# Two transformer blocks on one core: feed-forward stages in two phases, two matmuls per weight tile, later ada sums

## The reference

```python
def rmsnorm(x, g):
    y = xf * lax.rsqrt(jnp.mean(xf * xf, axis=-1, keepdims=True) + EPS)
def swiglu(h, w_in, w_out):                  # w_in 1024 x 5632, w_out 2816 x 1024
    a, b = jnp.split(h @ w_in, 2, axis=-1)
    return (jax.nn.silu(a) * b) @ w_out
...
x = x + 0.5 * swiglu(rmsnorm(x, g[0]), ffn_w_in[layer, 0], ffn_w_out[layer, 0])
```

```python
ada = c_act @ w_ada[l] + b_ada[l]            # 1024 x 6144 weights for one row
sh1, sc1, gt1, sh2, sc2, gt2 = [t[:, None, :] for t in jnp.split(ada, 6, axis=-1)]
...
u = x * (1.0 + sc2) + sh2
h = jnp.square(jax.nn.relu(u @ w_up[l])) @ w_down[l]
x = layer_norm(DN_ALPHA * x + (1.0 + gt2) * h, ln_ffn_g[l], ln_ffn_b[l])
```

## Time and profile before

| | us |
|---|---|
| median of 3 runs (lowest, highest) | 2049.49 (2048.72, 2058.34) |
| the profiled execution, its own time | 2051.69 |
| its span | 2050.0 |
| TensorE busy, weight loads busy | 1924.4, 1826.6 |
| VectorE, ScalarE, GpSimd busy | 1331.9, 919.0, 772.9 |
| mean granted clock of TensorE | 0.937 |

### The profile page before, as it was taken

How to read it: one execution, slowest core, us unless ns; L and a number is a source line. 1 busy time by engine, 2 the same in 40 slices (tenths; PEclk the granted TensorE clock), 3 DMA queues, 4 the chain that set the end, 5 groups by cost and what they waited for, 6 DMA issues and landing times.

```text
span 2050.0 us, 34772 instructions
## 1 busy us (share of the span) xinstructions
PE 1924.4 (94%) x14460; PEld 1826.6 (89%) x14460; DVE 1331.9 (65%) x1393; ACT 919.0 (45%) x1168; POOL 772.9 (38%) x392
## 2 busy tenths in 40 slices
PE   7999999889989999989799989998999899989998
PEld 7999896789989999875699988888999898889997
DVE  6876544567677767465677757966655579666554
ACT  5433454344334433444344334674544456645443
POOL 3967200136666657012346683950000039400000
PEclk9999896789999999895899999999999999999999
DMA  7878351356875777430367754434455444345551
GB/s 234 266 228 268 100 165 62 103 171 225 266 251 165 246 247 245 144 103 1 103 206 248 243 189 144 133 115 144 144 184 184 144 145 145 104 144 166 184 183 42
DMA packets 288106, 347.61 MB, mean 170 GB/s; under 512 B 15060, under 2 KB 263688, under 8 KB 288008
## 3 DMA queue, kind: packets, MB, share of 16 engines
q1 hardware_dynamic: 287976, 346.18, 52.2%
q10 hardware_dynamic: 32, 0.02, 0.0%
HBM read 345.11 MB, written 1.07 MB: 169 GB/s over the span
## 4 chain that ended last, share of the span: by engine, by line
PE 84%; DVE 9%; ACT 3%; issue 2%; SPq 1%; DMA 1%; DVEq 0%; ACTq 0%
PE bank L765 24%; PE bank L766 24%; PE bank L767 24%; DVE wl L1597 2%; PE bank L940 2%; ACT wh L1244 2%; PE bank L963 2%; PE bank L951 1%; PE bank L802 1%; PE bank L1140 1%; PE bank L1201 1%; DVE xl L1608 1%; DVE xn L1628 1%; DVE hl L1658 1%; DMA raw<-in_ffn_w_in 1%
## 5 line engine op out<-in xcount | busy, mean ns | idle before, releaser
L1597 DVE TENSOR_TENSOR wl<-raw,wh 128x2048 fp32r<-128x2048 f32 x275 | 729.1, 2656 | 390.3 <-ACT wh L1244 390.0
L765 PE MATMUL bank<-xh,wh 128*128 128x256 f32 x3056 | 886.2, 290 | 67.3 <-DVE xl L1608 34.6
L766 PE MATMUL bank<-xl,wh 128*128 128x256 f32 x3056 | 877.9, 287 | 0.0
L767 PE MATMUL bank<-xh,wl 128*128 128x256 f32 x3056 | 877.3, 287 | 0.0
L1244 ACT ACTIVATE wh<-raw 128x2048 fp32r<-128x2048 f32 x275 | 524.9, 1909 | 400.8 <-PE bank L767 381.3
L765 PEld LDWEIGHTS bank<-xh,wh 128*128 128x128 f32 x3056 | 599.8, 196 | 83.5 <-issue 51.2
L766 PEld LDWEIGHTS bank<-xl,wh 128*128 128x128 f32 x3056 | 600.4, 196 | 0.4 <-issue 0.2
L767 PEld LDWEIGHTS bank<-xh,wl 128*128 128x128 f32 x3056 | 599.8, 196 | 0.0
L707 POOL TENSOR_TENSOR arena<-arena,csil 128x2048 f32<-128x2048 f32 x48 | 190.8, 3975 | 507.3 <-DMA arena<-in_w_ada 488.0
L765 PE MATMUL bank<-hh,wh 128*128 128x256 f32 x1216 | 347.4, 286 | 17.0 <-DVE hl L1658 17.0
L767 PE MATMUL bank<-hh,wl 128*128 128x256 f32 x1216 | 347.1, 285 | 0.0
(11 more groups left out here) (254 smaller groups left out, 1659.7 us busy)
## 6 DMA issues: line engine op xcount, KB each, us to landing
raw<-in_ffn_w_in SPq DMA_DIRECT2D x88, 1024.0 KB, 5.8
arena<-in_w_ada SPq DMA_DIRECT2D x48, 1024.0 KB, 7.5
raw<-in_ffn_w_out SPq DMA_DIRECT2D x44, 1024.0 KB, 5.1
raw<-in_w_in SPq DMA_DIRECT2D x36, 1024.0 KB, 5.0
raw<-in_w_up SPq DMA_DIRECT2D x32, 1024.0 KB, 5.7
raw<-in_w_down SPq DMA_DIRECT2D x32, 1024.0 KB, 4.9
raw<-in_even_w_in SPq DMA_DIRECT2D x12, 1024.0 KB, 5.3
raw<-in_w_out SPq DMA_DIRECT2D x8, 1024.0 KB, 5.3
```

The lines of the kernel that those rows point to most:

```text
L765: pe.matmul(o, wa, ma, start=start, stop=False, **kw)
L766: pe.matmul(o, wa, mb, start=False, stop=False, **kw)
L767: return pe.matmul(o, wb, ma, start=False, stop=stop, **kw)
L1597: dve.tensor_tensor(wl[:, c % RING, :], raw[:, c % RING, :], wh[:, c % RING, :].bitcast(F32), ALU.subtract).then_inc(lo_made.sem, 1)
```

## The change

It rewrites the feed-forward stages and what touches them.

1. xh and xl become the halves of one tensor xx (k, half, token), and the split hidden values go to a tensor hx (22 or 32 tiles, two halves) which lies where the arena begins. A weight tile takes two matmuls (`pair`): the low weights times the high half (256 columns), and the high weights times both halves at once (512 columns). Results fill the left and the right half of a bank.
2. The right halves must be added: ScalarE copies them out (L1339, L1344), VectorE adds the left halves from PSUM (L1700, L1703), then product, and split into hx.
3. All up chunks of a stage come first, then the down chunks in four groups of 256 output columns (8 + 8 + 6 tiles of k in ffn, 8 + 8 + 8 + 8 in sq). After a group VectorE adds the left and then the right halves to x; ScalarE squares these two tiles of x, and TensorE adds them to the norm's sums after the second chunk of the next group (`pe_stats`), so that 2 of 8 remain for the end.
4. `pool_ada` starts when the last xl of the norm is made. The ada chunks are loaded in steps 1 to 6, 8 and 10 and one with each down group, so the last later than before. The rope inputs are loaded after all hl and ada sums of ffn3.
5. `fetch` runs a small activation so that the table for Sqrt or Silu is there before its use.
6. In the odd stage chunk 0, small and chunk 1 come before the transposes of wuk, and wuk is loaded there. The constants of the even stage move out of the arena. The clearing of hpad moves from the rope stage into the mix stage. PE waits in ffn2 for ada_made before its second chunk.

The other stages keep `three`.

```diff
@@ pe_ffn
+            def pair(o, k, hi_w, lo_w, halves, start, stop):
+                pe.matmul(o[:, 0:T], lo_w, halves[:, 0, :], start=start, stop=False, skip_group_check=True)
+                return pe.matmul(o.rearrange("p (h t) -> p h t", h=2), hi_w, halves, start=False, stop=stop, skip_group_check=True)
...
                 if st > 0:
-                    pe.wait_ge(h_made.sem, shifted(h_made.at(s, 2 * st), turn, 2 * body))
+                    pe.wait_ge(a_made.sem, shifted(a_made.at(s, st), turn, STEP_BODY))
+                up(c, st, turn, 4)
+                if st > 0:
+                    pe.wait_ge(b_made.sem, shifted(b_made.at(s, st), turn, STEP_BODY))
+                elif s == "ffn2":
+                    pe.wait_ge(ada_made.sem, ada_made.at("ffn1"))
+                up(c + 1, st, turn, 6)
...
+            for g, j, c, k0, n in down_chunks(s):
+                pe.wait_ge(lo_made.sem, c + 1)
+                if g == 0:
+                    pe.wait_ge(hl_made.sem, hl_made.at(s, min(4 * (j + 1), steps)))
+                if g >= 2 and j == 0:
+                    pe.wait_ge(x_ready.sem, x_ready.at(s, 2 * (g - 1)))
+                for m in range(2):
+                    for k in range(n):
+                        last = pair(bank[2 * (g % 2) + m], k0 + k, *tile_of(c, k, m, T), hx[:, k0 + k, :, :],
+                                    start=(k0 + k == 0), stop=(j == len(DOWN[KIND[s]]) - 1 and k == n - 1))
+                last.then_inc(chunk_used.sem, 1)
+                if g >= 1 and j == 1:
+                    pe_stats(NEXT[s], range(2 * g - 2, 2 * g))
@@ pool_ada
+            moving = {"ffn0": "rms0", "ffn1": "rms2", "ffn2": "rms3", "ffn3": "rms5"}[s]
+            pool.wait_ge(xl_made.sem, xl_made.at(moving))
@@ act_rms
+        def fetch(func):
+            act.activation(early[:, :], epsc[:, 0:1], func)
...
+            if s != "rms0":
+                fetch(ACT.Sqrt)
...
+            if KIND[NEXT[s]] == "ffn":
+                fetch(ACT.Silu)
@@ act_ffn
+                act.wait_ge(chunk_used.sem, shifted(c + 1, turn, per))
+                act.activation(ra, psum[:, 4:6, T:2 * T], ACT.Copy).then_inc(right_out.sem, 1)
                 hi(c + RING, turn, per)
+                act.wait_ge(a_made.sem, shifted(a_made.at(s, st + 1), turn, STEP_BODY))
+                act.activation(fs, ra, ACT.Silu).then_inc(act_made.sem, 1)
+                act.wait_ge(chunk_used.sem, shifted(c + 2, turn, per))
+                act.activation(rb, psum[:, 6:8, T:2 * T], ACT.Copy).then_inc(right_out.sem, 1)
+                hi(c + 1 + RING, turn, per)
+                act.wait_ge(h_made.sem, shifted(h_made.at(s, st + 1), turn, STEP_BODY))
+                act.activation(hx[:, mine, 0, :], fh, ACT.Copy).then_inc(hh_made.sem, 1)
@@ odd stage
-    ODD = ["wuk", 0, "small", 1, "index", 2, "csq", "top", 3, "cnorm", "top", 4, "top", "K", 5, "top", "V", "mask", 6]
+    ODD = [0, "small", 1, "wuk", "index", 2, "csq", "top", 3, "cnorm", "top", 4, "top", "K", 5, "top", "V", "mask", 6]
@@ rope stage, vector
-                dve.wait_ge(rope_made.sem, 4)
-                dve.memset(hpad[:, :, 0:CONV_K - 1], 0.0)
```

More of the change, by code:

```diff
@@ L445, in att_of, with steps_of @@
                     lambda h, b: Vm[:, b, h * HD:(h + 1) * HD], lambda h: bm[:, h % 3, :])
-    def steps_of(eng, n, head, body, step):
-        turns = (n - head) // body
+    NEXT = {s: n for (_, s), (_, n) in zip(STAGES, STAGES[1:])}
+    def steps_of(eng, s, step):
+        steps, head, body, tail = (FF_STEPS, 2, 3, 3) if KIND[s] == "ffn" else (FF2_STEPS, 4, 3, 3)
+        turns = (steps - head - tail) // body
         for i in range(head):
@@ L538, in sp_ffn @@
             w_out = w_out.rearrange("(k p) n -> p k n", p=P)
-            def step(i, st, turn):
-                c = c0 + (0 if st == 0 else n_in + (n_in + 1) * (st - 1))
-                per = (n_in + 1) * body
-                for half in range(n_in):
-                    load(c + half, columns(w_in, i * 256 + half * FF), A_VIEW, turn, per)
-                if st > 0:
-                    load(c + n_in, w_out[:, bass.ds(i * 2 - 2, 2), :], B_VIEW, turn, per)
             def load_ada(n, slot, times):
@@ L795, in pe_table @@
             pe.wait_ge(root_made.sem, 1)
[L796 removed]
+            pe.matmul(bank[0][0:16, 0:BIAS_COLS], bt[0:32, 0:16], bt[0:32, 16:16 + BIAS_COLS], start=True,
                       stop=True).then_inc(setup_pe.sem, 1)
         def pe_rms(s):
[L800 to L802 removed]
@@ L803, in pe_rms, with pe_stats @@
-            last.then_inc(stat_made.sem, 1)
+            pe_stats(s, range(6 if KIND.get(x_of[s]) == "ffn" else 0, KT))
+        def pe_stats(s, tiles):
+            for k in tiles:
+                if KIND[s] == "rms":
+                    pe.wait_ge(sq_made.sem, sq_made.at(s, k + 1))
+                else:
+                    pe.wait_ge(x_ready.sem, xr(s, k))
+                src = xn if KIND[s] == "rms" else x
+                last = pe.matmul(bank[STAT][:, 0:T], ones[:, :], src[:, k, :], start=(k == 0), stop=(k == KT - 1))
+            if tiles[-1] == KT - 1:
+                last.then_inc(stat_made.sem, 1)
@@ L1194, in pe_ln @@
         def pe_ln(s):
-            for k in range(KT):
-                pe.wait_ge(x_ready.sem, xr(s, k))
-                last = pe.matmul(bank[6][:, 0:T], ones[:, :], x[:, k, :], start=(k == 0), stop=(k == KT - 1))
-            last.then_inc(stat_made.sem, 1)
+            pe_stats(s, range(6 if s[3] == "b" else 0, KT))
             for k in range(KT):
```

347 lines of the change are left out of this document (179 added, 168 removed).

## The result

The changed kernel takes 2022.13 us (median of four runs, 2015.18 to 2030.28). The kernel before, with one more run than was shown above, takes 2053.16. The ratio is 0.984 (0.982 to 0.987). So the change gains 1.6%. The forecast was 1972 with a range of 1920 to 2013: the sign was right, but the gain was less than half of what was forecast, and the time lies outside the range. The profiled execution took 2024.51, its span is 2022.6, so 27.4 us less than the span before.

The account below looks back on a forecast made before the run. The prediction took TensorE's own work to be the bound, with its stops adding to the span. Its terms, -75 - 26 - 28 + 56 - 3 - 2 + 1.5, summed to -77 us, giving 1972 us, range 1920 to 2013.

Parts of the forecast that it names:

- the pair: Feed-forward stages: a 256- and a 512-column matmul per weight tile take 0.336 us, 0.024 less, over 3136 tiles: -75 us.
- stops for hl, h and their half clock: TensorE's waits for the last hl (17.0 us) and h (3.0 us) go, with the lowered clock behind hl stops: -26 us.
- first chunk of ffn1 and ffn3: With GpSimd's sums after the last xl, this chunk takes 7.5 to 8 us instead of 22.1: -28 us.
- shared turn in the up phase: VectorE and GpSimd alternating make steps 13.3 us against TensorE's 10.75, 14 us in each of four ffn stages: +56 us.
- norm sums per column group: Ends of six stages: 12 of 16 records leave the tail, which takes 3.3 us instead of 3.6: -2 us.
- rope: Stretch after ffn3: the last ada sum ends earlier, so the 20 us of rope tables start earlier: -3 us (0 to -6).
- odd stage, ffn2's wait: TensorE waits in ffn2 for ada_made (up to 1 us); the odd stage's first chunk runs at lower clock (0.5): +1.5 us.
- (a): Rival, ffn stages: the sums hide, VectorE's delays stay within the slack, 2 us a stage; 1924 us, chance 0.20.
- (c): Rival, ffn up phase: the alternation of VectorE and GpSimd holds for all 11 steps; 2012 us, chance 0.11.
- (b): Rival, feed-forward stages: the pair gains nothing, the excess of 0.013 us being per column; 2023 us, chance 0.11.
- (d): Rival, feed-forward stages: the 512-column matmul runs at two cycles per column, 0.43 us; slower, near 2600 us, chance 0.03.

Follow-up runs that it names:

- e1: The changed kernel with matmuls of 64 to 512 columns added behind its last product; full-clock starts 0.227 us apart at 512 columns, 0.120 at 256.
- e5: The kernel before with only GpSimd's wait for the last xl of the norm added ahead of the ada sums; 2025.4 us, ratio 0.984.
- e3: The changed kernel with GpSimd's long ada-sum work cut to 8 columns, so results are incomplete; 1988.65 us in a single execution.
- e7: The changed kernel with VectorE's addition of a's halves placed ahead of the low part of the step before; 2018.7 us, ratio 0.981.
- e9: The changed kernel with the odd stage's bias loads issued behind weight chunk 6, with the value weights, not ahead of chunk 5; 2016.5 us, ratio 0.981.
- e10: The changed kernel with the three rope loads issued behind the mix stage's third weight chunk, not ahead of its first; 2019.5 us, ratio 0.982.
- e11: The changed kernel with all norm products at the stage end, ada loads spread over the steps, odd-stage and rope loads later; 1992.6 us, ratio 0.969.

## Why the forecast was wrong, point by point

| term | forecast us | measured us |
|---|---|---|
| the pair | -75 | -32, by 3136 x (0.3599 - 0.3497) |
| stops for hl, h and their half clock | -26 | -28.1 |
| first chunk of ffn1 and ffn3 | -28 | -26.6 |
| shared turn in the up phase | +56 | +23.6: 19.4 of waits, the rest around them |
| norm sums per column group | -2 | +15.7, and 2.6 behind ffn0 |
| rope | -3 | +2.7 |
| odd stage, ffn2's wait | +1.5 | +6.3 and +0.6 |
| start, both mixes, small ends | 0 | +7.8 |
| sum | -77 | -27.4 (the spans: -27.4) |

The time of a stage is taken apart by the starts of neighbouring tiles: what each start lies beyond 0.36 us (before) or 0.35 us (after) goes to the first chunk, to the norm's records, to the stops or to the slow tiles behind them. The stops for hl and h cost 22.0 us before and the slow tiles behind them 6.9; 0.8 of it is left.

**The pair: the step that failed first.** The prediction took the 0.12 us of the earlier trace rows to be the weight load's floor, since the one-column matmul of the earlier trace rows needs 0.112, and let a long matmul hide its load. e1 shows two separate things: a floor of 0.11 for short matmuls, and about 0.013 us on top of the columns for every other one. 256 columns lie just above where the floor ends, so both readings gave 0.12 there. The half-clock spacing of 0.213 could not tell them apart: in e1 it is the columns of 256 and the floor at that clock alike. And the row taken for a long matmul was of another type: the float32 records of the earlier trace rows, of 1024 cycles, start 0.429 us apart, only 0.002 above their cycles, while the float32r ones of e1 have the 0.013. A pair saves one such extra and not the 0.024 us: 0.010 were measured, 32 us in place of 75. The price lay within the bounds named (0.325 to 0.36), but the value taken was far from it. The Trainium skill's formula (TensorE: Matmul & The Clock Gate, section "Back-to-back issue gap"), N / 2.4 + 2.5 ns, gives 216 ns at 512 columns; e1 has 227. By that formula the pair would have gained an estimated 8 us, by the prediction 75, and 32 came: neither had the 0.013 us.

**Stops and first chunks: right.** Both terms held within some 2 us, and e5 shows the second on its own.

**The shared turn: right mechanism, oversized.** e3 shows that GpSimd makes the waits, e7 that the one other order of VectorE that was tried doesn't cure them. GpSimd in ffn1 of the changed kernel, and VectorE's low part and addition:

```profile
420.70 5.66 POOL L740 TENSOR_TENSOR arena<-arena,csil 128x2048 f32<-128x2048 f32 x1
433.59 5.65 POOL L740 TENSOR_TENSOR arena<-arena,csil 128x2048 f32<-128x2048 f32 x1
446.46 5.65 POOL L740 TENSOR_TENSOR arena<-arena,csil 128x2048 f32<-128x2048 f32 x1
```

```profile
422.82 4.09 DVE L1709 TENSOR_TENSOR hx<-arena,hx 128x512 fp32r<-128x512 f32 x1
426.83 0.68 DVE L1700 TENSOR_TENSOR arena<-bank,arena 128x512 f32<-128x512 f32 x1
```

A turn lasts 12.9 us (forecast 13.3). The product, 3.6 us alone, is 5.66 long, because it begins while VectorE makes a low part; VectorE's own 0.7 us lasts 4.09. The addition reads PSUM and takes 0.68 like a lone one, as the earlier trace rows had it for L1653. But TensorE's step is 11.2 us and not 10.75, since the pair is dearer, and each stop is 1.6 us and not 2.55; and they are 5, 4, 1 and 4 in the four stages, not 5 or 6 in each: in ffn2 GpSimd stood idle for 6.1 us, until its fifth chunk had landed. Two errors of opposite sign hid each other here: had the pair been as cheap as forecast, these stops would by the same sum have been longer. The Trainium skill (SBUF — State Buffer, section "Who interferes with whom") calls the port pair of these two engines an exclusive lock for the whole instruction; the 4.09 agrees.

**The norm sums: the second step that failed.** The prediction compared the end of a stage before and after (3.6 and 3.3 us), took -2 us from it and forgot the 12 records that it had moved; they cost 15.7 us. On the engine that bounds the kernel, moved work costs its full time at its new place; at the old one it had filled a wait. It also missed that the emptied end is a stop, behind which, after ffn0, the clock fell. It had itself priced this effect for the hl stops.

**Odd, rope, the small ends.** The odd stage was forecast by TensorE's order alone. SyncE's queue decided: the bias load, which waits for the transposes, and the value weights' held up the chunks behind them (e9). In the rope stretch the prediction saw the tables, 20 us; they took 24 (first to last GpSimd record 1180.4 to 1204.5), and the next weights were held up in SyncE's queue behind the rope loads, which was worth little: without it the stretch is 1.5 us shorter (e10). The 6 us in the two mix stages are open: GpSimd's convolution additions (L779) take 1.36 us in the median where they took 1.10 (1.88 and 1.52 in the mean), with buffers at other addresses, but no run tested it. The start differs by the 1.3 us of the table, and goes from 20.5 to 23.0 us in the traces of the experiments.

**The rivals.** None is what happened. (a) is excluded by the 14 stops. (c) is excluded by their number. (b) named 2023, next to the measured 2022, but for another reason: it had a pair that gains nothing. (d) is excluded by the spacing of 0.23 us. The range ended at 2013 because no case had the norm sums or the loads in it.

## What to carry to other kernels

Ask of each part of a change whether it removes work from the bounding engine or only moves it: here the one line that kept GpSimd off a short serial stretch gave, alone, as much as the whole change, and moving products out of a wait into a full phase cost their whole time, 16 us. Two matmuls on one weight tile save a fixed extra per matmul, some 0.013 us, and not the time of a load. And follow every queue past which a step is moved: the odd stage's loss sat in SyncE's order. Taking back this, the rope loads' place, the norm sums and the bunched loads made 1.6% into 3.1%.

## What was new about the hardware

The pair's spacing has two levels, 0.347 and 0.353 us (832 and 848 cycles of 2.4 GHz), each for tens of microseconds at a time, both with a granted clock of 1.00. sq0 ran at the upper one in the changed kernel, sq1 mostly at the lower, with the same code. Means over an execution went from 0.3487 (e9) to 0.3522 us (e11), which is 11 us over 3136 tiles; the changed kernel's runs spread over 15 us, but only one of them was traced. Three matmuls of 256 columns in the kernel before stay at 0.360. What sets the level is open. In e1, pairs of 128 and 512 columns took 0.340 us, about the 0.111 and the 0.227 that each takes among its like.

The extra goes with the type: float32r matmuls of 512 columns start 0.227 us apart, float32 records of as many cycles (L843, 256 columns at two cycles each) 0.216.

And e1 shows a fall of the clock without a stop of TensorE: at 2058.04 us, behind matmuls of 128 and then 64 columns that had started every 0.11 us without a break, it went from 1.00 to 0.50, and came back at 2068.28 us, among those of 512 columns.
